# Taking out the products of constants between mixer and experts, and between the layers

## The reference: what is computed

```
x = layer_norm(ALPHA * x + gate1 * token_mixing(x * (1 + scale1) + shift1))
x = layer_norm(ALPHA * x + gate2 * hier_moe(x * (1 + scale2) + shift2))
```

## Time and profile before

| what | value |
|---|---|
| median of the three timed runs | 1540.84 us |
| the profiled execution, its own time | 1537.58 us |
| span of its trace, first to last instruction | 1535.8 us |
| mean granted TensorE clock | 0.975 |
| PE busy | 1406.4 us, 92% of the span |
| DVE busy | 591.1 us, 38% |
| ACT busy | 250.9 us, 16% |
| POOL busy | 170.9 us, 11% |
| HBM | 247 GB/s over the span |

### The profile page before, as it was taken

How to read it: one execution, slowest core, us unless ns; L and a number is a source line. 1 busy time by engine, 2 the same in 40 slices (tenths; PEclk the granted TensorE clock), 3 DMA queues, 4 the chain that set the end, 5 groups by cost and what they waited for, 6 DMA issues and landing times. The chain is left out here.

```text
span 1535.8 us, 17336 instructions
## 1 busy us (share of the span) xinstructions
PE 1406.4 (92%) x6534; PEld 693.7 (45%) x6534; DVE 591.1 (38%) x1100; ACT 250.9 (16%) x468; POOL 170.9 (11%) x140
## 2 busy tenths in 40 slices
PE   6879989989999899999986999899899989999994
PEld 2335445444445444444432454454444454444441
DVE  1233444422134433434452434443312453443535
ACT  0121211222201011111112112202211111111110
POOL 0123042011100000000003221501110000000000
PEclk9989999999999999999998999999999999999997
DMA  9624634644441899999872445245345079999992
GB/s 383 277 117 178 260 143 159 239 178 184 194 185 61 359 391 374 391 390 372 340 284 108 178 189 194 117 163 207 150 172 216 33 296 379 387 395 373 389 392 95
DMA packets 40255, 379.80 MB, mean 247 GB/s; under 512 B 7946, under 2 KB 12170, under 8 KB 17292
## 3 DMA queue, kind: packets, MB, share of 16 engines
q1 hardware_dynamic: 31776, 375.83, 61.5%
q10 hardware_dynamic: 8428, 3.29, 0.8%
HBM read 374.76 MB, written 4.33 MB: 247 GB/s over the span
## 5 line engine op out<-in xcount | busy, mean ns | idle before, releaser
L906 PE MATMUL psum<-ring,hT 128*128 128x512 f32 x1152 | 520.1, 600 | 13.7 <-DVE rows L1563 8.1
L906 PEld LDWEIGHTS psum<-ring,hT 128*128 128x128 f32 x1152 | 214.2, 192 | 256.2 <-issue 248.6
L1017 PE MATMUL psum<-ring,tbuf 128*64 128x256 f32 x2048 | 236.0, 384 | 4.8 <-DVE tbuf L1683 4.8
L1017 PEld LDWEIGHTS psum<-ring,tbuf 128*64 128x64 f32 x2048 | 145.5, 138 | 111.7 <-issue 42.3
L1044 PE MATMUL psum<-ring,tbuf 128*64 128x512 f32 x512 | 116.9, 598 | 1.0 <-ACT tbuf L1296 1.0
L1557 DVE TENSOR_TENSOR ch<-psum,bias_ring 128x512 f32<-128x512 f32 x68 | 46.8, 689 | 175.9 <-PE psum L906 175.9
L1689 DVE TENSOR_SCALAR tbuf<-tbuf 128x256 f32<-128x256 f32 x32 | 9.4, 294 | 214.4 <-ACT tbuf L1286 214.4
L1710 DVE TENSOR_TENSOR ch<-ch,psum 128x512 f32<-128x512 f32 x128 | 79.3, 681 | 17.2 <-PE psum L1055 13.1
L930 PE MATMUL psum<-ring,tbuf 128*128 128x512 f32 x192 | 82.9, 593 | 0.0
L1842 POOL TENSOR_SCALAR ldata<-ldata 128x512 f32<-128x512 f32 x24 | 46.1, 1920 | 281.1 <-ACT ldata L1242 281.1
L1055 PE MATMUL psum<-tbuf 64*128 64x512 f32 x256 | 63.6, 615 | 1.6 <-ACTq L524 1.6
(11 more groups left out here) (268 smaller groups left out, 1243.8 us busy)
## 6 DMA issues: line engine op xcount, KB each, us to landing
ring<-in_stream SPq DMA_DIRECT2D x162, 2048.0 KB, 9.6
bias_ring<-in_b_in SPq DMA_DIRECT2D x36, 256.0 KB, 8.3
ldata<-in_ldata SPq DMA_DIRECT2D x2, 2329.0 KB, 24.6
ch<-in_stream SPq DMA_DIRECT2D x2, 2048.0 KB, 25.4
hbuf<-in_ln SPq DMA_DIRECT2D x4, 1024.0 KB, 7.2
hbuf<-row_mem SPq DMA_DIRECT2D x4, 1024.0 KB, 6.3
hbuf<-in_stream SPq DMA_DIRECT2D x1, 2048.0 KB, 8.3
tbuf<-in_stream SPq DMA_DIRECT2D x1, 2048.0 KB, 11.6
```

The lines of the kernel that those rows point to most:

```text
L906: mm = pe.matmul(bank(PJ + g), hT[:, k, g * P:(g + 1) * P], w[:, k, :], start=(k == 0), stop=(k == KT - 1))
L1017: mm = pe.matmul(psum[halves_of[hf], j, 0:FE // 2], xgT[:, k, :], w_up(j)[:, k, hf * (FE // 2):(hf + 1) * (FE // 2)], start=(k == 0), stop ...
```

## The change

All calls of `hold_clock` and the function itself are taken out: ten products in each layer and seven between the layers, 27 in all. Nothing takes their place.

```diff
-                def hold_clock(n):
-
-                    for _ in range(n):
-                        pe.matmul(bank(5), ident, const[:, 0:W], start=True, stop=True)
-
                 out_proj(0, 0)
                 out_proj(0, 1)
                 out_proj(1, 0)
...
                 x_turned(l, 1, 0)
                 route(0)
                 tokens_back(0)
-                hold_clock(3)
                 turn_x(l, 1, 1, 6)
-                hold_clock(2)
                 x_turned(l, 1, 1)
                 route(1)
                 tokens_back(1)
-                hold_clock(5)
 
                 pe.wait_ge(sent_ready, l + 1)
...
                 further_passes(pe, expert_pass(0), expert_pass, no_pass)
 
-                if l + 1 < DEPTH:
-                    hold_clock(7)
                 pe.wait_ge(spread_added, step(l, PASSES, 0) * 4)
```

## The result

The changed kernel took 1549.87 us (median of five timed runs, 1548.25 to 1551.29) where the kernel before took 1540.73 us beside it: a ratio of 1.0061, 95% interval 1.0046 to 1.0076, or 9.1 us more. The forecast was 1548.5 us. The profiled execution took 1550.38 us, its span is 1548.6 us, and its mean granted clock is 0.952 where it was 0.975.

What follows compares the result with a forecast made beforehand. TensorE, busy 92% of the span, was taken as the bound. Terms 6.2 + 0.6 + 1.1 = +7.9 us on the median 1540.84 gave 1548.7, taken as 1548.5 us; range 1542.0 to 1556.0.

Steps and rivals of the forecast that it cites:

- The products delay nothing but the rank products: In both layers, the removed products hold up only the rank products, by about 0.4 us a layer.
- The clock falls in the gap ahead of the second transposition or soon after, in both layers: Clock falls between 491.5 and 495, mostly staying at half to the up products; transposition +0.3 us a layer, bounds 0 and 0.7.
- Routing 3.6 us, rank products 2.2, gather 3.6: Durations at half clock; routing +1.65, rank products +0.65, gather with its transposition +0.5 us a layer after cover.
- First up products: +0.6: Low clock expected at the up products of both layers, 3.4 us lost against 2.83 before; bounds -2.8 and +3.2.
- Between the layers: +1.1: Clock at half when x comes after 9.5 us idle: transposition +0.7, projection +0.4 us.
- The delays add: After the changed stages, neither POOL's chain in layer 1 nor expert slots absorb the delays; they reach the end.
- Late fall: Short work keeps the clock up until the idle time behind 498.0, transposition and routing cost nothing: +4.0, 1544.8 us; chance 0.2.
- No fall: From 489.5 to 502 the clock stays full, rank products come 0.4 us a layer sooner: -0.8, 1540.0 us; chance 0.09.
- absorbed: Clock falls, but later work waits anyway for expert slots or POOL; about 1 to 2 us left, 1542.5 us; chance 0.08.
- The sum: All changed stages of both layers and between them: 6.2 + 0.6 + 1.1 = +7.9 us, added to the median 1540.84.

Runs made afterwards that it cites:

- the first five experiments: Against the kernel before: only the 3 and 2, only the 5, only the 7, small products, few wide ones; 1544.7, 1553.3, 1547.35, 1553.06, 1543.71 us.
- the first one: Kernel before with only the 3 and 2 products around the second transposition of x kept, the 5 and 7 left out: 1544.7 us, ratio 1.0030.
- the second: Kernel before with only the 5 products ahead of the rank products kept: 1553.3 us, ratio 1.0082.
- the fourth: Kernel before with 6, 3, 8, 13 products of 16 columns, or 1, 1, 2, 3 of 512, in the same gaps: 1553.06 and 1543.71 us.
- the kernel whose five end 0.6 us late: Against the kernel with all waits filled: 5 products instead of 4 ahead of the rank products, one more ahead of the gather; 1525.8 us, ratio 0.9904.
- the one with four: Kernel before with 4 products instead of 5 ahead of the rank products, others added where the clock fell, POOL waits filled: 1526.83 us, ratio 0.9911.

## Why the prediction was right

- *The products delay nothing but the rank products.* Right: without them TensorE stands idle where they were. The rank products of the changed kernel start 0.06 us after DVE's L1627 (505.47 + 0.19), against 0.66 us behind its counterpart before.
- *The clock falls in the gap ahead of the second transposition or soon after, in both layers.* Right, and earlier in the stretch than I had weighed. I took 0.3 us for the transposition, as if it would mostly run before the fall; it took 1.97 and 1.92 us instead of 1.09, +0.9 and +0.8. That is the term that was mis-sized in this stage; its bound of 0.7 was too low as well, since 1.79 us was not the longest such row (2.07 stood beside it).
- *Routing 3.6 us, rank products 2.2, gather 3.6.* Measured 3.58, 2.32 and 3.68. The transposition behind the gather took 1.12 us (+0.46 for +0.45), and DVE's copy now waits for TensorE, as said. From routing to rank products the stretch grew by 1.04 us for the 1.25 forecast (1.65 less the 0.4 gained). The stage cost 3.66 and 3.61 us for the 3.1 forecast.
- *First up products: +0.6.* Measured +1.46 (0.10 and 1.36): the clock was low in both layers, and in layer 0 it came back after 5.9 us and not after the mean of 4.0. The term was too small.
- *Between the layers: +1.1.* Measured +2.12: 0.9 for the transposition instead of 0.7, and 1.24 instead of 0.4 for the projection, where the clock was low for about 6 us (791.91 to 797.9) and not for the mean.
- *The delays add.* Right. The starts of the same groups differ by 5.41 us after the first up products and by 5.53 at the end of the experts of layer 0, by 7.65 at 801.71 and by 7.80 at the output projection of layer 1. Neither the expert slots nor POOL's chain absorbed anything.
- *Late fall.* Out: the clock was at half at the second transposition of x, after an idle gap of 2.68 us. *No fall* is out by the same row, *absorbed* by the starts just given.
- *The sum* was 7.9 us; the two traces have 10.85 in the stages of the change, the medians 9.1. Adding the sum to the median and not to the quicker profiled execution was what brought the forecast near: from 1537.58 it would have been 1545.5. That choice was sound: the seven profiled executions that run the same instructions up to the first routing of layer 0 (both kernels and the first five experiments) reach it between 486.87 us, the kernel before, and 491.20, so that execution was early by chance. That a sum 3 us short of the traces missed the medians by only 1.2 us is in part luck, since single executions differ by as much.

What only the experiments show: that each gap is priced by what stands behind it (the first one), that products behind a fall that has already come bring nothing back (the second), and that wide products held the clock where small ones did not (the fourth).

## What to carry to other kernels

Price an idle gap of TensorE by the work behind it at the granted clock, up to the next long dense stretch, and not by the gap: here 23 us of products that nobody reads were worth 9 us, and 15 more came from filling the waits that the first tuning had left. Put such products right ahead of the real work, use wide ones, and start before the clock has fallen: five late ones took up to 6.09 us in place of 4.46 and held up what they should help. Whether they should rather end before the work is ready is not shown: the kernel whose five end 0.6 us late is as fast as the one with four. And look at more than one execution, as the seven products between the layers held the clock in four traces and not in two.

## What the hardware showed that I had not expected

A busy TensorE alone did not keep or bring back the clock. Routing and transposing back kept it busy for 5.35 of 5.36 us at half (changed kernel, 497.70 to 503.06) and the clock did not return; with small products added it was 8.6 us. Between the layers the clock fell under small products that ran without a break (784.20 to 785.00). In the stretches of the earlier trace rows dense work of 256 or 512 columns ran at half for 2.83 to 5.98 us before the clock came back. Nor do such wide products have to be there: in the kernel before, products and transpositions of 128 columns alone ran at half, and the clock was full again when the next projection began:

```profile
239.23:242.62 3.39, 3.39 (x16) 3.39 (x17) 1.28 (x2) 0.00 (x0) 1.24 (x1) 0.50 0.00 0
242.62:244.00 1.38, 1.38 (x5) 0.68 (x4) 0.74 (x2) 0.96 (x2) 0.50 (x2) 1.00 0.00 0
```

The Trainium skill's page "TensorE: Matmul & The Clock Gate", section "Part 1: The HAM clock gate (the "warmup" mystery)", says that the gate goes by how busy TensorE has been recently; by the trace's own busy share these stretches disagree, and the measurement decides.
